# Grouped attentions of a two-block transformer: probabilities streamed over held values, inverse totals laid out by products

## What is computed

```python
sc = jnp.einsum('bqkgd,bskd->bkgqs', qi, ki).astype(jnp.float32) * scale
sc = sc - slopes[:, :, None, None] * dist.astype(jnp.float32)
sc = jnp.where(valid, sc, -jnp.inf)
sink_col = jnp.broadcast_to(sink_f[None, :, :, None, None], sc.shape[:-1] + (1,))
p = jax.nn.softmax(jnp.concatenate([sc, sink_col], axis=-1), axis=-1)[..., :-1]
return jnp.einsum('bkgqs,bskd->bqkgd', p.astype(v.dtype), vi)
```

## Time and profile before

| what | value |
|---|---|
| time, median of 3 runs | 2526.25 us (2525.29 to 2527.48) |
| time of the profiled execution | 2525.54 us, of which the trace spans 2523.7 us |
| granted TensorE clock, mean | 0.998 |
| busy: PE / DVE / ACT / POOL | 2496.8 / 1189.6 / 947.5 / 182.6 us |
| PE's waits for DVE's bias ahead of a score (L783), whole run | 7.6 us in 6 waits |
| transfer of POOL's queue (`w_lo`, 512 KB), issue to landing | 4.4 us |
| attention a with its neighbours (60 to 165 us) | PE 101.19 of 105 us, ACT 71.17, DVE 49.32 |
| attention c0 with its neighbours (1115 to 1215 us) | PE 99.36 of 100 us, ACT 61.23, DVE 43.12 |

### The profile page before, as it was taken

The page is one execution under the profiler, slowest core; times in us unless marked ns, Lnnn a source line. Parts: engine busy times, 40 slices in busy tenths (PEclk is TensorE's granted clock), DMA queues, the critical chain, the costliest instruction groups (busy, mean ns, idle before and its releaser), DMA issues.

```text
span 2523.7 us, 28242 instructions
## 1 busy us (share of the span) xinstructions
PE 2496.8 (99%) x11504; PEld 2071.3 (82%) x11504; DVE 1189.6 (47%) x1595; ACT 947.5 (38%) x1398; POOL 182.6 (7%) x179
## 2 busy tenths in 40 slices
PE   9999999999999999999999999999999999999998
PEld 7878888888888888878888888888888788888887
DVE  6443454434475343454454444543444644544444
ACT  6668333322343232356432222422222464322222
POOL 2031010000020000011200000100000122000001
PEclk9999999999999999999999999999999999999999
DMA  7454433233223333245423332333332354332322
GB/s 197 109 124 118 134 108 100 92 100 101 92 84 109 93 99 94 89 130 130 115 95 100 93 99 89 99 97 99 94 101 87 112 142 117 100 99 93 100 90 78
DMA packets 78513, 265.33 MB, mean 105 GB/s; under 512 B 9648, under 2 KB 12976, under 8 KB 78000
## 3 DMA queue, kind: packets, MB, share of 16 engines
q1 hardware_dynamic: 69376, 233.57, 29.4%
q0 software_dynamic: 9008, 29.96, 6.0%
HBM read 234.56 MB, written 2.19 MB: 94 GB/s over the span
## 4 chain that ended last, share of the span: by engine, by line
PE 89%; DVE 4%; ACT 3%; issue 3%; POOL 0%; DMA 0%; SPq 0%; DVEq 0%; ACTq 0%; POOLq 0%
PE bank L769 28%; PE bank L770 28%; PE bank L771 28%; PE bank L810 2%; DVE w_lo L1091 2%; ACT w_hi L894 1%; PE bank L783 1%; PE bank L797 1%; DVE x L1207 1%; DVE z L1083 1%; ACT z L882 0%; POOL square_sum L1350 0%; DVE q L1158 0%; PE bank L843 0%; ACT h_hi L907 0%
## 5 line engine op out<-in xcount | busy, mean ns | idle before, releaser
L769 PE MATMUL bank<-h_hi,w_hi 128*128 128x512 f32 x2224 | 879.7, 396 | 2.7 <-DVE h_lo L1106 1.5
L771 PE MATMUL bank<-h_hi,w_lo 128*128 128x512 f32 x2224 | 867.2, 390 | 0.0
L770 PE MATMUL bank<-h_lo,w_hi 128*128 128x512 f32 x2224 | 867.0, 390 | 0.0
L1091 DVE TENSOR_TENSOR w_lo<-w_raw,w_hi 128x1024 fp32r<-128x1024 f32 (+2 forms) x392 | 485.3, 1239 | 318.3 <-ACT w_hi L894 317.9
L894 ACT ACTIVATE w_hi<-w_raw 128x1024 fp32r<-128x1024 f32 (+1 forms) x435 | 449.0, 1034 | 409.4 <-PE bank L771 407.3
L771 PEld LDWEIGHTS bank<-h_hi,w_lo 128*128 128x128 f32 x2224 | 417.9, 188 | 88.5
L769 PEld LDWEIGHTS bank<-h_hi,w_hi 128*128 128x128 f32 x2224 | 418.5, 188 | 86.9 <-DVE h_lo L1106 2.7
L770 PEld LDWEIGHTS bank<-h_lo,w_hi 128*128 128x128 f32 x2224 | 418.7, 188 | 80.8 <-issue 1.9
L769 PE MATMUL bank<-act_hi,w_hi 128*128 128x512 f32 x960 | 373.4, 389 | 0.0
L770 PE MATMUL bank<-act_lo,w_hi 128*128 128x512 f32 x960 | 373.4, 389 | 0.0
L771 PE MATMUL bank<-act_hi,w_lo 128*128 128x512 f32 x960 | 373.4, 389 | 0.0
(11 more groups left out here) (169 smaller groups left out, 1676.8 us busy)
## 6 DMA issues: line engine op xcount, KB each, us to landing
w_raw<-ffn_wg_dram SPq DMA_DIRECT2D x88, 512.0 KB, 3.5
w_raw<-ffn_wu_dram SPq DMA_DIRECT2D x88, 512.0 KB, 3.5
w_raw<-w_in_dram SPq DMA_DIRECT2D x67, 512.0 KB, 3.6
w_raw<-ffn_wd_dram SPq DMA_DIRECT2D x64, 512.0 KB, 3.5
w_lo<-w_raw POOLq DMA_DIRECT2D x51, 512.0 KB, 4.4
w_raw<-w_up_dram SPq DMA_DIRECT2D x32, 512.0 KB, 3.5
w_raw<-w_down_dram SPq DMA_DIRECT2D x32, 512.0 KB, 3.5
w_raw<-w_out_dram SPq DMA_DIRECT2D x24, 512.0 KB, 3.5
```

The lines of the kernel that those rows point to most:

```text
L769: engine.matmul(to, w_hi[s][:, lhs], hi, start=k == 0, stop=False)
L770: engine.matmul(to, w_hi[s][:, lhs], lo, start=False, stop=False)
L771: product = engine.matmul(to, w_lo[s][:, lhs], hi, start=False, stop=job == "k_last")
L1091: engine.tensor_tensor(lo, value, hi.bitcast(F32), ALU.subtract).then_inc(signals[event].s, 1)
```

## The change

For attentions a, c0 and c1 (`GROUPED`); b stays as it was:

- `turn` now gives two tiles in fp32r: ACT copies the high part (`turned_a_hi`, `turned_hi`), and a new job `turn_lo`, one slot later, has DVE form the rest from the turn bank. The bank is free only after that.
- The values are kept as 128 columns: 64 high, 64 low (`v_lo`, a new DVE job).
- `multiply` holds this 128x128 tile of values still and streams the 512 probabilities of the 4 heads over it, once high, once low. The sum stands in the value bank as output by tokens, so it needs no transpose; the lower 64 partitions hold the share of the low values.
- `pair`, after each group: ACT copies the lower half of the bank (`square_sum` or `lower`), DVE adds it to the upper half into half of `y` (a part of `x` for a). The next group's first product waits for this.
- `invert`: DVE adds the sink and inverts as soon as the block's last exponentials are there, ACT widens the 8 inverses to 512 columns (`wide`, for a a part of `x`). `spread`: 4 plain float32 products with the identity lay them out by tokens in a turn bank. `weigh`: DVE multiplies `y` by it, ACT writes the high part to `qa` or `q`, and `y_lo` a slot later has DVE form the rest.
- `normalise` and `turn_out` are left out. The scratch for POOL's transfers is halved.

```diff
@@ Plan.run
+        elif job == "exps" and key[0] in GROUPED and key[2] == 1:
+            self.later(1, "invert", *key[:2])
+        elif job == "turn" and key[0] in GROUPED:
+            self.later(1, "turn_lo", *key)
+        elif job == "v_turn" and key[1] is None:
+            self.later(1, "v_lo", *key)
+        elif job == "multiply" and key[0] in GROUPED and key[3] == len(CHUNKS[key[0]][key[1]]) - 1:
+            self.add("pair", key[:3])
+            if key[2] == 1:
+                self.later(1, "spread", *key[:2])
+                self.later(2, "weigh", *key[:2])
+        elif job == "weigh":
+            self.later(1, "y_lo", *key)
...
-            self.later(at + delay + 2 * len(chunks) + 5, "turn_out", name, i)
+            if name == "b":
+                self.later(at + delay + 2 * len(chunks) + 5, "turn_out", name, i)
...
@@ turn_freed
-            return done({"v_turn": "v_copied", "turn": "turn_copied", "turn_out": "y_lo"}[job], key)
+            if job == "turn":
+                return done("turn_lo" if key[0] in GROUPED else "turn_copied", key)
+            if job == "v_turn":
+                return done("v_lo" if key[1] is None else "v_copied", key)
+            return done("weighed" if job == "spread" else "y_lo", key)
...
@@ tensor_program
+                    if name in GROUPED:
+                        if c == 0:
+                            at = value_at["paired", key[:3]]
+                            pe.wait_ge(*done(*plan.values[at - 1]))
+                            pe.wait_ge(*done(*values_need(name)))
...
+                        pe.wait_ge(*done("turn_lo", key))
+                        engine.matmul(value_bank[:, :], values[name][:, chunk, g, :], turned_hi[name][:, at, :], start=c == 0, stop=False)
+                        engine.matmul(value_bank[:, :], values[name][:, chunk, g, :], turned_lo[name][:, at, :],
+                                      start=False, stop=last).then_inc(signals["multiplied"].s, 1)
+                        continue
...
+                elif job == "spread":
+                    name, i = key
+                    at = turn_at[job, key]
+                    pe.wait_ge(*done("widened", key))
+                    pe.wait_ge(*turn_freed(at - 2))
+                    for t in range(GROUP):
+                        spread = engine.matmul(turn_bank[at % 2][:, t * P:(t + 1) * P],
+                                               wide_of[name][:, t * P:(t + 1) * P], identity[:, :],
+                                               start=t == 0, stop=True, skip_group_check=True)
...
@@ scalar_program
+                elif job == "pair":
+                    name = key[0]
+                    act.wait_ge(*done("multiplied", (*key, len(CHUNKS[name][key[1]]) - 1)))
...
+                    engine.activation(lower_of[name], value_bank[HEAD:P, :], ACT.Copy).then_inc(signals["lower_copied"].s, 1)
...
+                elif job == "weigh":
+                    name, i = key
+                    act.wait_ge(*done("weighed", key))
+                    engine.activation(y_hi_of[name][:, :, block(i)], y_of[name].rearrange("p (t n) -> p t n", t=4), ACT.Copy).then_inc(signals["y_hi"].s, 1)
...
@@ vector_program
+                elif job == "pair":
+                    v.wait_ge(*done("lower_copied", key))
+                    engine.tensor_tensor(y_of[key[0]][half(key[2]), :], value_bank[0:HEAD, :], lower_of[key[0]], ALU.add).then_inc(signals["paired"].s, 1)
...
+                elif job == "weigh":
+                    name, i = key
+                    v.wait_ge(*done("paired", (name, i, 1)))
+                    v.wait_ge(*done("turned", key))
+                    engine.tensor_tensor(y_of[name], y_of[name], turn_bank[turn_at["spread", key] % 2][:, :], ALU.mult).then_inc(signals["weighed"].s, 1)
...
-    nc = bacc.Bacc("TRN2", target_bir_lowering=False, num_devices=1, dynamic_dma_scratch_size=4096)
+    nc = bacc.Bacc("TRN2", target_bir_lowering=False, num_devices=1, dynamic_dma_scratch_size=2048)
```

More of the change, by code:

```diff
@@ L126 @@
         "score": ("scored", "biased"), "mask_bias": ("bias_half", "bias_masked"), "softmax": ("sink_shift",),
-        "exps": ("exped",), "turn": ("turned", "turn_copied"), "multiply": ("multiplied",),
-        "normalise": ("row_total", "row_inv", "normalised"), "turn_out": ("turned", "y_hi"), "y_lo": ("y_lo",),
+        "exps": ("exped",), "turn": ("turned", "turn_copied"), "turn_lo": ("turn_lo",), "multiply": ("multiplied",),
+        "pair": ("lower_copied", "paired"), "invert": ("row_total", "row_inv", "widened"), "spread": ("turned",), "weigh": ("weighed", "y_hi"), "v_lo": ("v_lo",),
+        "normalise": ("row_inv", "normalised"), "turn_out": ("turned", "y_hi"), "y_lo": ("y_lo",),
         "neg_sinks": ("neg_sinks",), "rel_bias": ("rel_spread",), "far_1": (), "far_2": (),
@@ L179, in run @@
             return
-        if job in ("turn", "turn_out", "v_turn"):
+        if job in ("turn", "turn_out", "v_turn", "spread"):
             self.turns.append((job, key))
-        if job == "multiply" and key[2:] == (0, 0):
+        if job == "multiply" and key[0] in GROUPED and key[3] == 0:
+            self.values.append(("paired", key[:3]))
+        if job == "multiply" and key[0] == "b" and key[2:] == (0, 0):
             self.values.append(("normalised", key[:2]))
@@ L681, in two_blocks @@
         chunk_at = {key: n for of in plan.chunks.values() for n, key in enumerate(of)}
+        paired_before = {}
+        for name in GROUPED:
+            of = [key for job, key in plan.values if job == "paired" and BUFFERS[key[0]] == BUFFERS[name]]
+            paired_before.update(zip(of[1:], of))
         def turn_freed(n):
@@ L1295, in vector_program @@
                                          ALU.mult).then_inc(signals["normalised"].s, 1)
+                elif job == "y_lo" and key[0] in GROUPED:
+                    name, i = key
+                    v.wait_ge(*done("y_hi", key))
+                    rest(y_lo_of[name][:, :, block(i)], y_of[name].rearrange("p (t n) -> p t n", t=4), y_hi_of[name][:, :, block(i)], "y_lo")
                 elif job == "y_lo":
```

95 lines of the change are left out of this document (69 added, 26 removed).

## The result

The changed kernel takes 2543.06 us (median of 4 runs, 2540.99 to 2544.16) against 2525.77 us of the kernel before (4 runs, 2524.97 to 2527.48). The ratio is 1.0067, its 95% interval 1.0055 to 1.0079: **17.3 us slower**. Ratios are taken over fast runs; one launch of e8 took 5351.29 us and is the only slow one. The profiled execution spans 2542.1 us, 18.4 more than before.

What follows compares the result with a forecast made beforehand. PE's queue was taken to bound the kernel; -15.6 us of PE's work, +24.7 of waits in a and +4.2 in c0 and c1 gave +13.3, rounded to +12.3: 2538.5 us, range 2522 to 2551.

Steps and rivals of the forecast that it cites:

- PE's own work, -15.6: Attentions a, c0, c1: cheaper multiplies take out 21.1 us, dearer spread adds 5.5, so PE's work falls by 15.6 us.
- Rival D: Long products of multiply 0.13 us dearer each than dense ones, 12.5 us on 96 products: 2551 us; chance 0.03.
- The two long waits, +7.2 and +6.7: Attention a: PE waits 7.2 us for a bias at score (1, 1, 2), and 6.7 more at score (3, 0, 2).
- Rival A: Pair's copy on ACT comes before the backlog, so both long waits and their follow-ups go: 2518 us; chance 0.12.
- Small waits of a: Shorter waits in attention a at multiplies, turns and biases, such as 1.0, 1.4, 1.4 and together 7.25 us.
- the six places of blocks 2 and 3: Attention a: turn_lo or the bias late behind qb's copies and the split of weights, 0.35 to 2.75 us, together 7.25.
- the gain of 1.0 at b's first scores: A longer lead of DVE ends a wait of b's first scores, taking 1.0 us off the sum for a.
- rival B: Long waits come as forecast but small ones fall into PE's lateness: -0.3 us, 2526 us; chance 0.12.
- My rounding of 1 us: About 1 us off the sum, since a wait that makes PE late shortens the next: +13.3 to +12.3.
- c0 and c1, -4.3 + 2.1 each: Each c: PE's work falls 4.3 us; waits of 1.8 us at a score and multiplies, with v_lo 2.1, are added.
- Rival C: Mixers c as tangled as a, with 5 to 6 us more of waits in each: 2550 us; chance 0.14.
- The start and what was costed at nothing: v_lo ahead of scores costs 0.7 us; ACT's copies and widenings, some 30 DVE operations and the halved scratch cost nothing.

Runs made afterwards that it cites:

- e8: The change with only ACT's order altered beside attention a: exponentials and splits of weights one slot later, DVE's order untouched; 2533.8 us, ratio 1.0032.
- e2: The kernel before with 11 superfluous rests of 64x512 on DVE ahead of kb_lo of tile 1; 2534.14 us, ratio 1.0033.
- e4: The change for mixers c0 and c1 alone, attention a as before, halved scratch kept; 2521.88 us, ratio 0.9985 to the kernel before.
- e1: The change with DVE's end-of-block work in attention a put later (addition five slots behind the last multiply), ACT's queue unchanged; 2530.5 us, ratio 1.0018.
- e5: e1 with the inversion of a's totals three slots behind the last exponentials instead of one; 2527.17 us, ratio 1.0007.
- e6: e5 with a's exponentials a slot later and the end of a block a slot earlier; 2531.31 us, ratio 1.0024.
- e7: e6 with the splits of weights beside attention a one slot later; 2527.71 us, ratio 1.0008.

## Why the prediction was right, and where its terms were off

Forecast +12.3 us, measured +17.3 (18.4 on the profiled execution): slower as said, and by the mechanism named. That the sum came so near is in part luck: the waits of a were reckoned some 5 us too high (1 us of it taken off in the rounding), and the clock, worth 6.5 us there, is missing. Term by term:

- **PE's own work, -15.6: right.** The long products start 0.23 us apart, and the products with the identity cost 0.90 us. The changed kernel's timeline at c0 (first a multiply, then a `spread` with the dense step ahead of it and behind it):

```profile
1163.46 0.39 PE L845 MATMUL bank<-turned_hi,v 128*128 128x512 f32 x1
1163.69 0.39 PE L846 MATMUL bank<-turned_lo,v 128*128 128x512 f32 x1
1163.92 0.40 PE L803 MATMUL bank<-h_hi,w_hi 128*128 128x512 f32 x1
1164.16 0.39 PE L804 MATMUL bank<-h_lo,w_hi 128*128 128x512 f32 x1
1164.38 0.40 PE L805 MATMUL bank<-h_hi,w_lo 128*128 128x512 f32 x1
1164.62 1.05 PE L867 MATMUL bank<-identity,wide 128*128 128x128 f32 x8
1165.43 0.47 PE L803 MATMUL bank<-h_hi,w_hi 128*128 128x512 f32 x1
1165.74 0.39 PE L804 MATMUL bank<-h_lo,w_hi 128*128 128x512 f32 x1
```

  From 1163.46 to 1163.92 is 0.46 for two products; 1165.74 - 1164.38 - 0.46 = 0.90 as reckoned for the multiply in the earlier trace rows. Rival D falls. The Trainium skill (TensorE: Matmul & The Clock Gate, "The mechanism") has a load of the held tile overlap only when it goes to other rows of the array, by which the prediction had estimated half the gain; these starts do not agree with it either. One figure beside the term is wrong as recorded: were the products with the identity twice as dear (1.80 us), they would add 12 x 1.36 = 16.3 us, not 10.8.
- **The two long waits, +7.2 and +6.7: right.** 7.08 us, and 7.51 where 1.37 stood, +6.1. The walk through the queues gave both places, the chain and its order; DVE stood idle 8.20 us ahead of the pair, which started 6.4 us after its product's end (83.75). Rival A did not happen; made by hand in e8, it took away 5.0 and 3.0 us of the two waits, not all, since I had priced it with the bias in time.
- **Small waits of a: too large.** The brackets of the timeline give multiply (0, 0, 0) +1.0 as said, turn (1, 1, 1) +0.9 instead of +1.4, multiply (1, 1, 1) nothing instead of 1.4, the six places of blocks 2 and 3 3.7 us (1.46, 1.74, 0.49 and three times none) instead of 7.25, and the gain of 1.0 at b's first scores did not come (1.71 us of waits there, 1.63 before). The part of rival B was real: behind a wait PE is late and finds the next thing ready. My rounding of 1 us for that was about 4 too small.
- **Missing: the clock, 6.5 us in a.** I counted a wait as its length. Behind three of them PE ran at 0.50: from 96.99 to 101.3, 114.9 to 118.3 and 146.3 to 152.5 us, 13.9 us in all. A product takes 0.43 there instead of 0.23, so 0.20/0.43 of that time is lost, 6.5 us. This nearly closes the sum for a: waits 22.6 - 3.8 = +18.8, work -7.0, clock +6.5 make +18.3, measured 19.5. e2 shows the price alone, in the kernel before. This is the step that failed: the sum of waits, in which no term stood for what the engine does behind them. The trace of before could have told it: its longest wait for a bias, at one of the first scores, is followed by a stretch at half clock (55.0 to 58.4 us), in which the dense products start 0.43 us apart (56.13, 56.55, 56.98).

```profile
53.71 0.38 PE L783 MATMUL bank<-ka_hi,qa 128*128 128x256 f32 x1 [3.48 <-DVE neg_max L1270]
...
57.00:58.00 1.00, 1.00 (x4) 0.81 (x3) 0.00 (x0) 0.99 (x4) 0.09 (x1) 0.50 1.15 225
```

- **c0 and c1, -4.3 + 2.1 each: nearly right.** From the starts of the same dense products, c0 and c1 are 1.9 and 2.0 us shorter, with the rest of v counted in; forecast 2.2. The brackets show only 1.4 us more of waits in each (0.64 at the first scores, 0.43 and 0.31 at two multiplies), but by those starts PE lost 2.4 in c0. A bracket counts from the modelled end of the record ahead, which is 0.39 us long where products start 0.23 apart, and so undercounts every short wait; at the multiply of 0.43 the loss was 0.72. Some of the 1.2 us by which the sum for a falls short must be this. Rival C falls.
- **The start and what was costed at nothing.** The change reaches 61 us 1.6 us late, of which I had 0.7. The shifts give three parts: 0.4 is there at 30 us, before anything of the change runs (the other kernels lie between -0.9 and +0.3 there); 0.6 comes with the rest of v, which stands on DVE just ahead of the evacuation at 44 us, and makes PE's first long wait for a bias end at 54.75 instead of 53.71; 0.6 more is the clock, which around the end of that wait stands at 0.50 from 53.5 to 60.3 us where before it did from 55.0 to 58.4. In e4, with the old a and the halved scratch, nothing is late there, so it is not the scratch.

## What to carry to other kernels

When an edit ties two engines together at several points, walk both queues in order at each such point: what stands ahead on the other engine, and what stands behind on this one. The price is then mostly set by where the small jobs are put: here the same operations made the kernel 0.67% slower or 0.27% faster. A long wait of PE costs more than its length, 1.7 us on top of 6.3 here, so removing one is worth more than the list of waits says, while short waits behind a long one are worth less. Before you sum up new waits, look in the trace that you have at the granted clock behind its longest one.

## What the runs showed of the hardware

The granted clock can fall while PE waits and is not back when its work is. With 6.30 us of idle in e2 the products were 0.43 us apart for 3.3 us behind it, with 7.08 us in the changed kernel for 4.3 us, with 7.51 us for 6.2 us. The fall can also come after the wait: with 3.48 us in the kernel before, the first three products behind it still start 0.23 us apart, and 0.50 stands from 1.3 us behind its end on (55.0 to 58.4). Beside attention a, waits of 1.2 to 1.8 us were followed by 1.00. Those of 2.1 to 2.5 us went either way: 0.50 behind 2.12 and 2.53 (e8), 2.28 (e1), 2.29 twice (e5) and 2.54 us (the change), 1.00 behind 2.39, 2.28 and 2.27 (e6), 2.29 and 2.25 us (e7). What decides between them stays open. Over attention a the mean was 0.91, and PE's busy time over the whole run fell by 4.7 us where its work had fallen by 15.6: busy time of PE is no measure of its work when the clock differs. The Trainium skill (TensorE: Matmul & The Clock Gate, Part 1) has the clock at half rate after idleness and gives matmuls of 512 columns a start-to-start of 426.7 ns cold and 215.7 ns warm; the rows here agree with the first at 0.43 us and stand a little above the second at 0.23.
